# A one-core mixture-of-experts block: the two smallest of experts 2 to 7 as one fp32 job of 64 plus 64 slots

## The chip, the cores and the metric

The kernel runs on one core of one Trainium2 chip. The metric is the device time of one execution in microseconds, as the median of several runs. The profile is that of one execution, taken by the hardware profiler.

## What is computed

Four layers act on 256 tokens of 1024 features, all in fp32: a gated convolution and LRU mixer with a dense SwiGLU, the same mixer with a mixture of experts (MoE), an SSD and linear-attention layer, and an attention layer. The change touches the mixture of experts only:

```python
def moe_swiglu(h, w_router, wg, wu, wd):          # h: 256 x 1024
    logits = (xt @ w_router).astype(jnp.float32)   # 8 experts
    top_v, top_i = lax.top_k(logits, TOP_K)        # TOP_K = 2
    gates = jax.nn.softmax(top_v, axis=-1)
    ...
    for e in range(N_EXPERTS):                     # N_EXPERTS = 8, D_FF = 3584
        y = y + comb[:, e:e + 1] * swiglu(xt, wg[e], wu[e], wd[e])
```

Every token chooses two of eight experts, so 512 rows are spread over the experts. Worked out from the reference on its own inputs, experts 0 to 7 get 66, 73, 63, 66, 66, 56, 56 and 66 rows. The gate, up and down weights of one expert are 1024 x 3584, 1024 x 3584 and 3584 x 1024, 44 MB in all.

## The kernel before

**Pieces.** All weights come through one ring, `raw`, of RAW = 6 slots of 128 x 2048 fp32, one MiB each; a transfer of one MiB is called a piece here. SP issues the transfers in one order. `load` (L222 and on) lets SP wait until the piece six places earlier has been split (`w_lo`). ACT copies a piece in two halves to `whi`, rounded to fp32r (L558), and DVE subtracts to get the remainder `wlo` (L1079). `whi` and `wlo` have SPL = 3 places, so ACT can be three pieces ahead of TensorE, no more: it waits for `w_used`. `three` (L1848) then makes each product of three fp32r matmuls: high by high, high by low, low by high. For an expert a matmul has 128 slots as its stationary operand and 512 weight columns moving, so a piece costs 4 x 3 = 12 matmuls.

**Experts.** `gather` (L2101, L2102) picks up to 128 rows of each of two experts by one-hot matmuls, so a pair of experts is one `job_pair` of PU = 84 pieces. The hidden features are worked in blocks of 1024, 1024, 1024 and 512 (`FEAT`), eight steps to a pair. In step n TensorE does the gate pieces (banks 0 and 1), turns the hidden rows of the step before (`turn_h`, L2148, through banks 6 and 7), does the up pieces (banks 4 and 5), and then the down pieces of the step before (banks 2 and 3). ACT applies silu (L761) and evicts, DVE multiplies. Pieces of a 1024-wide block and all down pieces have runs of 4 KB in memory, those of the 512-wide gate and up blocks 2 KB.

**Order of the experts.** Pairs (0,1), (2,3), (4,5) and (6,7) run in this order, the last in a loop whose count is read from `tab`; an expert with more than 128 rows would add jobs to that loop. The results of jobs 0 to 3 are stored to `y_rows` in DRAM by GpSimd's queue (L488), fetched back by row number (L497) and added to X by DVE (L1441). Those of jobs 4 to 7 are scattered by one-hot matmuls (L2167, L2168). GpSimd works out the overflow and row tables (`overflow`, `two_rows`, L437 to L482).

**Elsewhere.** Three places of the trace show operations that resemble the new ones: `chunk_state` (L2289) and `att_out` (L2522, L2523) are plain fp32 matmuls of 128 x 64 stationary operands whose outputs go to partitions 0 to 63 and 64 to 127, and the router's logits (L2072) are fp32 matmuls of 8 columns, followed by `keep_busy` (L1968), which repeats transposes while DVE ranks the logits.

Of the kernel before, what the change touches and what calls it, by code (L numbers as in the profile page):

```python
# [24 lines left out]
P = 128  # L25
# [9 lines left out]
NJMAX = 12  # L35
# [18 lines left out]
STORED = 4  # L54
# [24 lines left out]
GATE, UP_, DOWN = step_units()  # L79

# [4 lines left out]
def build(nc, a, out):  # L85
    with ExitStack() as ctx:
# [40 lines left out]
        tab = sb("tab", [P, 6], I32)  # L127
        srt = sb("srt", [P, 1024], F32R)
        row_of = sb("row_of", [P, 2 * NT], I32)
        y_rows = nc.dram_tensor("y_rows", (STORED * P, D), F32, kind="Internal").ap()  # L130
# [51 lines left out]
        RV, VM, CW, RT = ar(936, NT, NE), ar(952, NT, NE), ar(968, NT, NE), ar(984, NT, NE)  # L182
        ROW = ar(1000, NT, 2)
        w_loaded = [sem(f"w_loaded{i}") for i in range(RAW)]
        w_hi, w_lo, w_used = sem("w_hi"), sem("w_lo"), sem("w_used")

        def plus(c, k, d):
            return c if isinstance(d, int) and d == 0 else d * k + c

# [35 lines left out]
        def _(sp):  # L225
            def load(u, src):
                c, d = u
                if c >= RAW or not isinstance(d, int):
                    sp.wait_ge(w_lo, plus(2 * (c - RAW + 1), 12, d))
                dst = raw[:, c % RAW, :]  # L230
                if len(src.shape) == 3:
                    dst = dst.rearrange("p (k n) -> p k n", k=src.shape[1])
                sp.dma_start(dst, src).then_inc(w_loaded[c % RAW], 16)
# [89 lines left out]
            def job_pair(e0, e1, d):  # L323

                for n in range(STEPS):
                    e = (e0, e1)[n // 4]
                    for m, units in ((eg, GATE[n]), (eu, UP_[n])):
                        for i, c in enumerate(units):
                            load((U_MOE + c, d), columns(m, e, i, n))
                    if n:  # L330
                        e = (e0, e1)[(n - 1) // 4]
                        for i, c in enumerate(DOWN[n - 1]):
                            load((U_MOE + c, d), down_rows(e, i, n - 1))
                for i, c in enumerate(DOWN[STEPS - 1]):
                    load((U_MOE + c, d), down_rows(e1, i, STEPS - 1))

            for p in range(NE // 2):
                job_pair(2 * p, 2 * p + 1, p * (2 * NG))
            sp.wait_ge(sem("tab_ready"), 1)
            njobs = sp.value_load(tab[0:1, 4:5], min_val=NE, max_val=NJMAX)  # L340
            npairs = sp.value_load(tab[0:1, 5:6], min_val=NE // 2, max_val=NJMAX // 2)
            with sp.If(njobs > NE):
                sp.wait_ge(sem("r_over"), 1)
                with sp.Fori(NE // 2, npairs) as p:
                    e0 = sp.value_load(tab[0:1, bass.ds(p * 2 - NE, 1)], min_val=0, max_val=NE - 1)
                    e1 = sp.value_load(tab[0:1, bass.ds(p * 2 - NE + 1, 1)], min_val=0, max_val=NE - 1)
                    job_pair(e0, e1, sp.snap(p * (2 * NG)))
# [34 lines left out]
        def _(pool):  # L382
# [45 lines left out]

            def overflow():

                pool.wait_ge(sem("r_log"), 1)
                pool.memset(TF[:, 0:4], 0.0)
                pool.memset(COMB[:, :, 11:14], 0.0)
                link(pool.memset(POS[:, :, 11:14], -1.0))
                pool.wait_ge(sem("r_step"), 4)
                G = GT3[:, 0, :].rearrange("p (e f) -> p e f", e=NE)
                link(pool.tensor_tensor(G, OV.unsqueeze(1).to_broadcast([P, NE, NE]), LTM[:, :].rearrange("p (e f) -> p e f", e=NE), ALU.mult))  # L437
# [5 lines left out]

                total(OVR.unsqueeze(2), lambda u, v: G[:, :, u:v])
                for m in range(3):
# [3 lines left out]
                    link(pool.tensor_tensor(EX, T16, sel2, ALU.mult))  # L449
                    total(MX.unsqueeze(2), lambda u, v: EX[:, :, u:v])  # L450
                    link(pool.tensor_scalar(POS[:, :, NE + m], MX, -1.0 - P, None, ALU.add))
                    link(pool.tensor_tensor(EX, COMB[:, :, 0:NE], sel2, ALU.mult))
                    total(COMB[:, :, NE + m:NE + m + 1], lambda u, v: EX[:, :, u:v])
                    link(pool.tensor_tensor(T8, SEL, iot[:, 0:NE], ALU.mult))
                    total(TF[:, m:m + 1], lambda u, v: T8[:, u:v])
                pool.tensor_copy(tab[:, 0:4], TF[:, 0:4]).then_inc(sem("r_over"), 1)

            def two_rows():

                def total4(o, x):  # L460

                    link(pool.tensor_tensor(RT[:, :, 0:2], x[:, :, 0:2], x[:, :, 2:4], ALU.add))
                    link(pool.tensor_tensor(o, RT[:, :, 0:1], RT[:, :, 1:2], ALU.add))

                first, second = RV[:, :, 0:4], RV[:, :, 4:8]
                valid, ahead, row = VM[:, :, 0:4], VM[:, :, 4:8], CW[:, :, 0:4]
                link(pool.memset(ahead, 0.0))
                link(pool.tensor_scalar(valid, T16[:, :, 0:STORED], float(P), None, ALU.is_le))
                link(pool.tensor_tensor(valid, valid, CH[:, :, 0:STORED], ALU.mult))
                for e in range(1, STORED):  # L470
                    link(pool.tensor_tensor(ahead[:, :, e:e + 1], ahead[:, :, e - 1:e], valid[:, :, e - 1:e], ALU.add))
                link(pool.tensor_tensor(second, valid, ahead, ALU.mult))
                link(pool.tensor_tensor(first, valid, second, ALU.subtract))
                link(pool.tensor_scalar(T8, iot[:, 0:NE], float(P), None, ALU.mult))
                link(pool.tensor_tensor(row, T16[:, :, 0:STORED], T8[:, 0:STORED].unsqueeze(1).to_broadcast([P, NT, STORED]), ALU.add))
                for k, m in enumerate((first, second)):
                    link(pool.tensor_tensor(CW[:, :, 4:8], COMB[:, :, 0:STORED], m, ALU.mult))
                    total4(WGT[:, :, k:k + 1], CW[:, :, 4:8])
                    link(pool.tensor_tensor(CW[:, :, 4:8], row, m, ALU.mult))
                    total4(ROW[:, :, k:k + 1], CW[:, :, 4:8])  # L480
# [3 lines left out]
            def rows_out_and_back():  # L484
# [4 lines left out]
                pool.wait_ge(sem("htok_lo"), 2)  # L489
                for b in range(2):  # L490
                    pool.wait_ge(sem(f"y_stored{b}"), 8 * STORED)
                for i in range(NT):
                    if i:
                        pool.wait_ge(sem("r_step"), 4 + i)
                    for k in range(2):
                        m = 2 * i + k
                        pool.indirect_dma_start(HTOK[:, k, :], None, y_rows[:, :],  # L497
# [4 lines left out]
            for k in range(10):  # L502
# [11 lines left out]
                if k == 3:  # L514
# [3 lines left out]
                    pool.tensor_tensor(HTOK[:, 0, :], X[:, 0, :], BG, ALU.mult).then_inc(sem("x_gain0"), 1)  # L518
# [12 lines left out]
                if k == 3:  # L531
                    overflow()
                    two_rows()
                    rows_out_and_back()
# [5 lines left out]
        def _(act):  # L540
# [8 lines left out]
            def split(u):  # L549
                c, d = u  # L550
                if c >= U_END:
                    return
# [2063 lines left out]
```

## Time and profile before

| | us |
|---|---|
| median of 3 runs | 1774.19 (1773.51 to 1774.86) |
| the profiled execution | 1774.9 |
| span of its profile | 1773.0 |
| TensorE busy | 1743.2 (98%) |
| weight loads of TensorE busy | 1479.7 (83%) |
| VectorE busy | 1409.8 (80%) |
| ScalarE busy | 1154.8 (65%) |
| granted TensorE clock, mean | 0.994 |
| moved by the DMA engines | 487.29 MB |

The profile is read with the names PE for TensorE, PEld for its weight loads, DVE for VectorE, ACT for ScalarE, POOL for GpSimd and SP for SyncE. L1848 is line 1848 of the kernel. A matmul's duration includes its way through the array, so in a row of matmuls the distance of the starts is the cost. A plain fp32 matmul is recorded as two. The DMA share is the mean busy share of the core's 16 DMA engines and can exceed 1 a little.

### The profile page before, as it was taken

The numbers are of one execution on the slowest core, as the hardware profiler recorded it, in microseconds if no ns is written. First come the engines' busy times: TensorE is split into PE (matmuls) and PEld (weight loads), VectorE is DVE, ScalarE is ACT, GpSimd is POOL, SyncE is SP. The second block draws the span as 40 slices with busy tenths as digits, with TensorE's granted clock in tenths as the row PEclk, the third lists the DMA queues.
The fourth block names the chain that finished last, engine by engine and source line by source line (L and its number), as shares of the span: only waits on it lengthen the run. The fifth ranks groups of instructions, "written<-read, shape, count | busy, mean of one in ns | idle before, by whom it ended". The sixth has DMA issues, their size and how long they took to land.

```text
span 1773.0 us, 23586 instructions
## 1 busy us (share of the span) xinstructions
PE 1743.2 (98%) x9169; PEld 1479.7 (83%) x9169; DVE 1409.8 (80%) x1532; ACT 1154.8 (65%) x1365; POOL 83.1 (5%) x137
## 2 busy tenths in 40 slices
PE   7999999999999999999999999999999999999998
PEld 7988888898888888888888888888888798778886
DVE  8864455697899998999989999989999888656555
ACT  5644444464777777777777777777777647554554
POOL 0000000001800000000000000000000001000000
PEclk9999999998999999999999999999999999999999
DMA  9555555544899999999999999999999834435420
GB/s 337 165 182 190 189 189 190 167 161 152 316 375 386 388 375 353 377 370 376 383 351 409 364 390 373 368 351 359 370 375 364 308 120 145 140 125 164 164 96 36
DMA packets 162734, 487.29 MB, mean 275 GB/s; under 512 B 13413, under 2 KB 14644, under 8 KB 162628
## 3 DMA queue, kind: packets, MB, share of 16 engines
q1 hardware_dynamic: 160832, 480.02, 74.2%
q0 software_dynamic: 1152, 4.19, 0.6%
q8 instruction: 70, 1.15, 0.3%
q10 hardware_dynamic: 644, 1.63, 0.2%
q14 instruction: 36, 0.29, 0.0%
HBM read 482.67 MB, written 3.15 MB: 274 GB/s over the span
## 4 chain that ended last, share of the span: by engine, by line
PE 93%; DVE 4%; ACT 1%; issue 1%; DMA 0%; POOL 0%; POOLq 0%; DVEq 0%; ACTq 0%
PE ps L1848 85%; PE ps L2148 1%; DVE wlo L1079 1%; DVE arena L1520 1%; PE ps L2101 1%; PE ps L2102 1%; DVE arena L1070 1%; ACT whi L558 0%; PE ps L1940 0%; PE ps L1992 0%; PE ps L2320 0%; PE ps L2035 0%; PE ps L2072 0%; PE ps L2512 0%; DMA X<-in_x 0%
## 5 line engine op out<-in xcount | busy, mean ns | idle before, releaser
L1079 DVE TENSOR_TENSOR wlo<-raw,whi 128x1024 fp32r<-128x1024 f32 x910 | 1067.9, 1221 | 236.2 <-ACT whi L558 232.7
L558 ACT ACTIVATE whi<-raw 128x1024 fp32r<-128x1024 f32 x910 | 913.4, 1053 | 455.7 <-PE ps L1848 453.8
L1848 PE MATMUL ps<-whi,ya 128*128 128x512 f32 x2272 | 715.8, 391 | 2.7 <-DVE ya L1070 1.4
L1848 PEld LDWEIGHTS ps<-whi,ya 128*128 128x128 f32 x2272 | 426.6, 188 | 91.1 <-issue 1.9
L1848 PE MATMUL ps<-wlo,ya 128*128 128x512 f32 x1136 | 442.2, 389 | 0.0
L1848 PE MATMUL ps<-whi,yh 128*128 128x512 f32 x896 | 281.9, 390 | 0.2
L1848 PEld LDWEIGHTS ps<-wlo,ya 128*128 128x128 f32 x1136 | 213.4, 188 | 43.1
L1848 PEld LDWEIGHTS ps<-whi,yh 128*128 128x128 f32 x896 | 168.2, 188 | 36.2 <-DVE yh L1070 1.2
L1848 PE MATMUL ps<-hhi,whi 128*128 128x256 f32 x656 | 188.2, 287 | 2.2 <-DVE hlo L1141 1.8
L1848 PE MATMUL ps<-hlo,whi 128*128 128x256 f32 x656 | 185.6, 283 | 0.0
L1848 PE MATMUL ps<-hhi,wlo 128*128 128x256 f32 x656 | 185.5, 283 | 0.0
L1848 PE MATMUL ps<-wlo,yh 128*128 128x512 f32 x448 | 174.3, 389 | 0.0
L1848 PE MATMUL ps<-whi,hhi 128*128 128x512 f32 x352 | 140.6, 399 | 0.8 <-DVE hlo L1141 0.8
L1848 PE MATMUL ps<-whi,hlo 128*128 128x512 f32 x352 | 137.4, 390 | 0.0
L1848 PE MATMUL ps<-wlo,hhi 128*128 128x512 f32 x352 | 137.1, 390 | 0.0
L1848 PEld LDWEIGHTS ps<-hhi,whi 128*128 128x128 f32 x656 | 125.6, 192 | 5.0 <-issue 4.1
L1848 PEld LDWEIGHTS ps<-hlo,whi 128*128 128x128 f32 x656 | 125.8, 192 | 0.1
L1848 PEld LDWEIGHTS ps<-hhi,wlo 128*128 128x128 f32 x656 | 125.7, 192 | 0.0
L1848 PEld LDWEIGHTS ps<-wlo,yh 128*128 128x128 f32 x448 | 84.1, 188 | 17.3
L1848 PEld LDWEIGHTS ps<-whi,hhi 128*128 128x128 f32 x352 | 66.2, 188 | 16.4 <-issue 2.9
L1848 PEld LDWEIGHTS ps<-whi,hlo 128*128 128x128 f32 x352 | 66.1, 188 | 14.1
L1848 PEld LDWEIGHTS ps<-wlo,hhi 128*128 128x128 f32 x352 | 66.2, 188 | 12.7
(369 smaller groups left out, 1133.0 us busy)
## 6 DMA issues: line engine op xcount, KB each, us to landing
raw<-in_moe_w_gate SPq DMA_DIRECT2D x112, 1024.0 KB, 7.2
raw<-in_moe_w_up SPq DMA_DIRECT2D x112, 1024.0 KB, 7.1
raw<-in_moe_w_down SPq DMA_DIRECT2D x112, 1024.0 KB, 7.5
raw<-in_even_w_in SPq DMA_DIRECT2D x21, 1024.0 KB, 5.1
raw<-in_w_in SPq DMA_DIRECT2D x20, 1024.0 KB, 6.0
raw<-in_odd_w_in SPq DMA_DIRECT2D x16, 1024.0 KB, 5.2
raw<-in_ffn_w_gate SPq DMA_DIRECT2D x14, 1024.0 KB, 5.1
raw<-in_ffn_w_up SPq DMA_DIRECT2D x14, 1024.0 KB, 5.1
```

The costliest lines, as they stand in the source:

```text
L558: act.activation(hi_of(u)[:, n], raw[:, c % RAW, n], ACT.Copy).then_inc(w_hi, 1)
L1070: return dve.tensor_tensor(o, x, y, op)
L1079: dve.tensor_tensor(lo_of(u)[:, n], raw[:, c % RAW, n], hi_of(u)[:, n].bitcast(F32), ALU.subtract).then_inc(w_lo, 1)
L1520: ins = dve.scalar_tensor_tensor(CVV[:, q, :], XP[:, q, k:k + S], col(1, C_ECONV + 10 * k + q), CVV[:, q, :], ALU.mult, ALU.add)
L1848: ins = pe.matmul(o, s, m, start=first and n == 0, stop=last and n == 2, skip_group_check=True)
L2101: pe.matmul(o, TKh[:, i, P * c:P * (c + 1)], SR[:, i, :], start=i == 0 and c % 2 == 0, stop=False)
L2102: ins = pe.matmul(o, TKl[:, i, P * c:P * (c + 1)], SR[:, i, :], start=False, stop=i == 1 and c % 2 == 1)
L2148: ins = pe.transpose(ps[:, 6 + q // 4, P * (q % 4):P * (q % 4 + 1)], MHF[:, P * q:P * (q + 1)], ident[:, :])
```

## The change

The two experts of 2 to 7 with the fewest rows are found on the chip. The other four and experts 0 and 1 keep the old path: three pairs, 252 pieces, in the order of a table that GpSimd makes. The two small experts form a job B. Its 84 pieces take no split: TensorE reads them from `raw` as plain fp32. The rows of one small expert stand in slots 0 to 63, those of the other in slots 64 to 127; each is a stationary operand of 64 columns whose output goes to its own half of the PSUM partitions. Job B is cut into 21 phases of four pieces (two of each expert), put in between the parts of pairs 0 and 1 by a table, from piece 24 on, some 6.1 pieces of the pairs apart (in fact 2, 4, 6 or 8); the last one comes after piece 150. Both kinds of pieces share the ring of six, fetched strictly in order of use, and a slot that held a B piece is freed by TensorE (`b_used`).

The phases use banks 6 and 7, so `turn_h` moves to banks 4 and 5, and ahead of the gate pieces of the next step. STORED falls from 4 to 3 (jobs 0 to 2 are stored), and job B's result is added up in SBUF (`YACC`) and stored as a fourth block. `add_rows` now runs in one go after pair 1. GpSimd gets the ranking of the experts (`jobs`) and a reordering of the tables; the overflow check is now against 128 rows for the six and 64 rows for the two small ones, and extra pairs run if it is exceeded.

```diff
-NJMAX = 12
+NJ0 = 6
+NJMAX = 10
-STORED = 4
+STORED = 3
+SLOTS = 5
+PHASES = [(kind, g, h) for g in range(4) for kind in "gud" for h in range(2 if g < 3 else 1)]
+LAST_HALF = [g == 3 or h == 1 for _, g, h in PHASES]
+FIRST_PHASE, PHASE_SPACING = 24, 6.1
+def load_order():
+    order, ahead = [], {done - 1: f for f, done in PHASE_AT.values()}
+    for a in range(2 * PU):
+        order.append(("A", a))
+        if a in ahead:
+            order += [("B", 4 * ahead[a] + i) for i in range(4)]
+        def load_wait(k, d):
+            if isinstance(d, int) and 0 <= k - U_MOE < len(ORDER):
+                kind, i = ORDER[k - U_MOE]
+                return (b_used, i + 1) if kind == "B" else (w_lo, 2 * (U_MOE + i + 1))
+            return w_lo, plus(2 * ((k if k < U_MOE else k - NB) + 1), 12, d)
...
# SP
+            eb, pieces = None, pair_pieces(0, 1)
+            for k, (kind, i) in enumerate(ORDER):
+                if eb is None and (kind == "B" or i == PU):
+                    sp.wait_ge(sem("router_made"), 2)
+                    eb = expert(10), expert(11)
+                if kind == "B":
+                    fetch(U_MOE + k, 0, small_piece(i, eb))
+                    continue
+                if i == PU:
+                    pieces = pair_pieces(expert(6), expert(7))
+                load((U_MOE + i, 0), next(pieces))
...
# ACT
+                f = PHASE_AT.get(here, (None,))[0]
+                if f is not None and PHASES[f][0] == "g" and LAST_HALF[f]:
+                    act.wait_ge(b_used, 4 * (f + 1))
+                    act.activation(HBC[:, 0:w], ps[:, 6:6 + w // 512, :]..., ACT.Silu).then_inc(sem("h_evicted"), 1)
...
# DVE
             def add_rows(i):
-                dve.wait_ge(sem("y_back"), 32 * (i + 1))
+                dve.wait_ge(sem("y_back"), 64)
...
# PE
+            def small_gather(half):
+                for i in range(NT):
+                    for c in range(4 * half, 4 * half + 4):
+                        pe.matmul(o, TKh[:, i, P * c:P * (c + 1)], m, start=i == 0 and c % 2 == 0, stop=False)
+                        ins = pe.matmul(o, TKl[:, i, P * c:P * (c + 1)], m, start=False, stop=i == 1 and c % 2 == 1)
+            def small_in(f, g, h):
+                for i in range(2):
+                    got = small_units(f, i)
+                    for k in range(ks):
+                        kk = ks * (2 * h + i) + k
+                        for b in range(width // 512):
+                            for s in range(2):
+                                pr, o = slice(64 * s, 64 * (s + 1)), width * k + 512 * b
+                                ins = pe.matmul(ps[pr, 6 + b, :], XBC[:, kk, pr], got[s][:, o:o + 512], start=kk == 0, stop=kk == KD - 1,
+                                                skip_group_check=True)
+                    ins.then_inc(b_used, 2)
...
-                    moe_in(GATE[n], d, n, 0, t if n == 0 else None)
+                    if n > 1:
+                        turn_h(t, n - 1)
+                    moe_in(GATE[n], u0, d, n, 0, t if n == 0 else None, (t, 0) if n == 1 else None)
+                    if not loop:
+                        small((t, n, "g"))
                     if n:
-                        turn_h(t, n - 1)
-                    moe_in(UP_[n], d, n, 4)
+                        pe.wait_ge(sem("m_htlo"), plus(n, STEPS, t))
+                    moe_in(UP_[n], u0, d, n, 4)
+                    if not loop:
+                        small((t, n, "u"))
...
-            for pair in range(STORED // 2):
-                job_pair(pair, pair * (2 * NG), 2 * pair + 1, stored=(2 * pair, 2 * pair + 1))
-            job_pair(STORED // 2, STORED * NG, STORED + 1, written=STORED)
+            job_pair(0, U_MOE, 0, 0, 1)
+            job_pair(1, U_MOE + PU, 0, 2, 3)
```

`small` puts a phase behind a part of a step: it gathers the small experts' rows once (`small_gather`, in step 1 of pair 0), turns the hidden rows of job B four times, and runs `small_in` for gate and up phases and `small_down`, of the same form, for down phases.

## Rows read from the trace of the kernel before

**Rows 1.** Stretches of 100 us: busy time (instructions), granted clock, DMA share, GB/s.

```profile
core 0: us, PE busy (x) PEld busy (x) DVE busy (x) ACT busy (x) POOL busy (x), PEclk, DMA share, GB/s
500.00:600.00 100.00, 100.00 (x457) 83.07 (x456) 91.30 (x84) 78.15 (x80) 0.81 (x1) 1.00 1.00 383
```

**Rows 2.** The same of the four pairs, and of all that follows.

```profile
443.00:683.00 240.00, 239.74 (x1100) 199.59 (x1101) 214.83 (x191) 183.60 (x187) 40.34 (x68) 1.00 0.97 365
683.00:921.00 238.00, 237.97 (x1094) 198.10 (x1093) 215.41 (x192) 183.90 (x188) 1.08 (x2) 1.00 0.99 375
921.00:1162.50 241.50, 241.43 (x1109) 200.54 (x1109) 224.15 (x204) 184.52 (x188) 6.44 (x5) 1.00 0.99 376
1162.50:1406.00 243.50, 243.35 (x1118) 202.06 (x1116) 224.31 (x205) 184.75 (x189) 0.00 (x0) 1.00 0.97 360
1406.00:1773.00 367.00, 351.83 (x2347) 302.56 (x2347) 242.75 (x377) 200.84 (x347) 18.76 (x18) 0.99 0.39 127
```

**Rows 3.** The chain that ended last, in order of time: start, us, what.

```profile
443.22 32.95 PE ps L1848 x144
476.18 0.87 PE ps L2148 x8
477.05 32.66 PE ps L1848 x144
...
672.43 0.44 PE ps L2148 x4
672.86 0.12 PE ps L2101
...
676.64 38.38 PE ps L1848 x168
...
1400.15 5.76 PE ps L1848 x24
1405.93 1.03 ACT yb L769
```

**Rows 4.** Waits from 440 to 1400 us, and of SP's queue from 500 to 1380 us.

```profile
ACT whi L558 <- PE ps L1848: 218.8, 298, 3.5
DVE wlo L1079 <- ACT whi L558: 71.2, 176, 3.1
...
SPq L233 <- DVE wlo L1079: 763.5, 309, 6.9
```

**Rows 5.** DMA issues by tensor: count, KB, median us to landing.

```profile
raw<-in_moe_w_gate SPq DMA_DIRECT2D x112, 1024.0 KB, 7.2
raw<-in_even_w_in SPq DMA_DIRECT2D x21, 1024.0 KB, 5.1
...
y_rows<-arena POOLq DMA_DIRECT2D x4, 512.0 KB, 7.6
...
arena<-y_rows,row_of POOLq DMA_INDIRECT x4, 8.3
```

**Rows 6.** Stretches of 5 and 10 us, columns as in rows 1.

```profile
10.00:15.00 5.00, 4.59 (x24) 4.22 (x25) 5.00 (x10) 4.65 (x10) 0.00 (x0) 1.00 1.04 382
15.00:20.00 5.00, 5.00 (x44) 5.00 (x43) 5.00 (x6) 3.43 (x5) 0.00 (x0) 1.00 1.05 387
...
630.00:640.00 10.00, 10.00 (x46) 8.29 (x45) 8.87 (x8) 7.96 (x10) 0.00 (x0) 1.00 0.95 347
690.00:700.00 10.00, 10.00 (x46) 8.29 (x45) 8.57 (x9) 8.04 (x9) 0.00 (x0) 1.00 1.03 417
```

**Rows 7.** PE in order of time around the 64-column fp32 matmuls: start, us.

```profile
1482.09 1.08 PE L2289 MATMUL ps<-arena,gb 128*64 128x512 f32 x4 [0.20 <-DVE arena L1070]
1483.10 0.50 PE L1848 MATMUL ps<-whi,hhi 128*128 128x512 f32 x1
...
1670.37 0.66 PE L2522 MATMUL ps<-gb,arena 128*64 128x256 f32 x4
1670.85 0.40 PE L2523 MATMUL ps<-gb,arena 128*64 128x128 f32 x4
1671.18 0.39 PE L1848 MATMUL ps<-hhi,whi 128*128 128x256 f32 x1
```

**Rows 8.** Groups from 440 to 1400 us: xcount, busy, mean ns, idle before.

```profile
L441 POOL TENSOR_TENSOR arena<-arena 128x4 f32<-128x4 f32 (+2 forms) x10 | 5.7, 567 | 0.8
...
L1441 DVE SCALAR_TENSOR_TENSOR X<-arena,X 128x1024 f32<-128x1024 f32 x4 | 5.1, 1283 | 0.1
```

**Rows 9.** PE in order of time, the router's matmuls: start, us.

```profile
424.62 5.29 PE L2072 MATMUL ps<-gb,hTf 128*128 128x8 f32 x32 [0.46 <-ACT hTf L735]
```

**Rows 10.** A stretch of 10 us behind them, columns as in rows 1.

```profile
430.00:440.00 10.00, 9.44 (x43) 8.79 (x43) 8.20 (x31) 2.39 (x4) 1.12 (x4) 0.50 0.00 1
```

More of the change, by code:

```diff
@@ L341, in _ @@
[L341 to L347, printed above, removed]
+                        for i in range(len(DOWN[n - 1])):
+                            yield down_rows(e, i, n - 1)
@@ new lines, in pair_pieces, with small_piece, expert @@
+                for i in range(len(DOWN[STEPS - 1])):
+                    yield down_rows(e1, i, STEPS - 1)
+            def small_piece(b, eb):
+                kind, g, h = PHASES[b // 4]
+                i = 2 * h + b // 2 % 2
+                return down_rows(eb[b % 2], i, g) if kind == "d" else columns((eg, eu)[kind == "u"], eb[b % 2], i, g)
+            def expert(o):
+                return sp.value_load(tab[0:1, o:o + 1], min_val=0, max_val=NE - 1)
+            eb, pieces = None, pair_pieces(0, 1)
@@ L458, in two_rows, with total5 @@
             def two_rows():
-                def total4(o, x):
+                def total5(o, x):
                     link(pool.tensor_tensor(RT[:, :, 0:2], x[:, :, 0:2], x[:, :, 2:4], ALU.add))
[L463 to L480, printed above, removed]
+                    link(pool.tensor_tensor(RT[:, :, 0:1], RT[:, :, 0:1], RT[:, :, 1:2], ALU.add))
+                    link(pool.tensor_tensor(o, RT[:, :, 0:1], x[:, :, 4:5], ALU.add))
@@ L789, in job_pair @@
                     if n == 4:
-                        used(U_MOE + DOWN[n - 1][-1], d)
+                        used(u0 + DOWN[n - 1][-1], d)
                         y0()
+                    if n and not loop:
+                        small((t, n, "d"))
                 ht_hi(t, STEPS - 1)
                 gath_hi(plus(1, 1, t))
-                after(U_MOE + DOWN[-1][0], d)
-                used(U_MOE + DOWN[-1][-1], d)
-                y1()
-                after(U_MOE + DOWN[-1][-1], d)
+                after(u0 + DOWN[-1][0], d)
@@ L1455, in job_pair @@
-                    if not stored and n in (1, 5):
-                        done = earlier if n == 1 else j1
-                        if done is not None:
-                            scatter(done)
-                            dve.wait_ge(sem("m_sev"), done)
+                    after(u0 + GATE[n][early], d, len(GATE[n]) - early)
+                    if n == 1 and not loop and t == 0:
+                        small_onehot()
+                    if not loop:
+                        small((t, n, "g"))
@@ L1460, in job_pair @@
+                    after(u0 + UP_[n][0], d, len(UP_[n]))
+                    used(u0 + UP_[n][-1], d)
+                    hid(t, n)
+                    if not loop:
+                        small((t, n, "u"))
+                    if loop and n in (1, 5):
+                        done = j0 if n == 1 else j1
+                        scatter(done)
+                        dve.wait_ge(sem("m_sev"), done)
+                    if loop and n == 1 or (loop or t) and n == 5:
                         weights_of(j0 if n == 1 else j1)
-                    if n == 2 and stored:
-                        dve.wait_ge(sem("m_gth"), 2 * t + 2)
+                    if n == 2 and not loop and t == 0:
+                        dve.wait_ge(sem("m_gth"), 2)
@@ L2108, in moe_in @@
+            def moe_in(units, u0, d, n, bank, fresh=None, turn=None):
                 s = n // 4
@@ L2199, in job_pair @@
                     if n:
-                        moe_down(t, d, n - 1)
+                        moe_down(t, u0, d, n - 1)
+                    if n and not loop:
+                        small((t, n, "d"))
                 turn_h(t, STEPS - 1)
                 gather(plus(1, 1, t))
-                moe_down(t, d, STEPS - 1)
-            for pair in range(STORED // 2):
-                job_pair(pair, pair * (2 * NG), 2 * pair + 1, stored=(2 * pair, 2 * pair + 1))
-            job_pair(STORED // 2, STORED * NG, STORED + 1, written=STORED)
```

495 lines of the change are left out of this document (356 added, 139 removed).

## The prediction

> **What bounds the kernel now.** I read the stretches of the span first, then the chain, then the waits, then the DMA rows. In the stretch of the experts TensorE is busy all the time at the full clock, and so, nearly, are the DMA engines: share 1.00 at 383 GB/s [rows 1]. VectorE is at 91%, ScalarE at 78%. So TensorE is the bound, but there are two resources near their end, and a change that relieves only one is worth what the other allows.
>
> The chain confirms it: from 443.2 to 1405.9 us it is TensorE's own work, with three-term matmuls in rows of 144 and a turn of hidden rows between [rows 3]. 144 matmuls take 32.66 us, 0.227 us each, so a piece of 12 costs 2.72 us, and 84 pieces 228.7. The four pairs are 240, 238, 241.5 and 243.5 us long [rows 2]; the 10 to 15 us above 228.7 are turns (0.87 us for 8), the gather (672.9 to 676.6, 3.7 us) and scatters. The waits show who is late: ScalarE waits for TensorE (218.8 us), VectorE for ScalarE, SP's queue for VectorE's split; nobody waits for a transfer [rows 4]. But a transfer of the experts lands 7.2 us after its issue, where a similar one in the slack stage lands after 5.1 [rows 5]: there is already a short queue. 84 MiB in 238 us are 370 GB/s at a share of 0.99 [rows 2].
>
> The span is thus 443.2 (before the experts) + 962.7 (four pairs) + 367.1 (all after) = 1773.0. It is 1.9 below the time of the profiled execution (1774.9) and 1.2 below the median (1774.19), so I add 1.2 to a span.
>
> **What the change takes and gives on TensorE.** It takes out one pair and puts 21 phases of 16 fp32 matmuls of 512 columns in. The cost of one is seen in `chunk_state`, of exactly this form: two such matmuls, on the two column blocks, start at 1482.09, and the next instruction starts at 1483.10, so both together cost 1.01 us, with the way in and out [rows 7]. Four of `att_out`, 256 and 128 columns on each block, cost 0.81 us (1670.37 to 1671.18). The difference, 128 columns, is 0.20, so in a row 512 columns of both blocks cost 0.80 from this difference and at most 1.01. I take 0.86, nearer the slope because eight pairs follow each other, plus 0.2 once: 7.1 us a phase (bounds 6.6 and 8.1). `att_out` writes both halves into one bank, as the phases do. 21 phases: 149 us for work that cost 228.7 us as split pieces.
>
> Further on TensorE: `small_gather`, 32 matmuls like the gather's, 3.7 us; 28 more transposes at 0.87/8, 3.1 us; one pair's turns, gather and scatter go. If nothing else bound it, the span would be 443.2 + 478 (pairs 0 and 1) + 149 + 3.7 + 3.1 + 2.5 (below) + 243.5 (the loop's pair) + 367.1 = 1690. A gain of 83 us, the most there is.
>
> **What the transfers allow.** The bytes stay: 336 pieces. Until now each had 2.72 us of TensorE to hide behind; in the mixed stretch, 126 pieces of the pairs (24 to 150) and 84 of job B, TensorE would need 126 x 2.85 (238/84 with the turns) + 149 = 508 us for 210 pieces, 2.42 us each, or 433 GB/s. No row reaches that. What can the queue deliver when always full? From below: share 1 at whole pairs means 376/0.99 = 380 and 360/0.97 = 371 GB/s [rows 2]. From above: 417 in the best 10 us, though 347 in a bad one [rows 6]. A full queue shows in the kernel's first microseconds, 382 and 387 at shares of 1.04 and 1.05, with runs of 2 KB, where the experts have mostly 4 KB. I take 390 GB/s: a piece (1.0486 MB) takes 2.69 us, bounds 2.51 (417) and 2.83 (371).
>
> Whole pairs ran at 375 and 376 GB/s [rows 2]. The Trainium skill, "DMA: Bandwidth & Descriptors", Specifications, gives about 358 GB/s as what one core can have from its memory and 435 as the ceiling of the fabric. By the first figure 206 pieces would take 604 us and the time below would be some 1790 in place of 1741; these two pairs already disagree with it, and no row comes near the second.
>
> The ring does not starve the engines in this state. While TensorE runs the last split piece ahead of a phase, SP can issue nothing from the second split piece behind the phase until two B pieces are used, about 3 x 2.72 + 3.5 - 2.3 (a split, ACT then DVE) = 9.4 us; but when transfers are the bound, five of six slots are under way then, over 13 us of transfer.
>
> The sum: 443.2; pieces 0 to 23, 24 x 2.72 = 65.3; two turns, 1.7; `small_gather` 3.7: TensorE reaches the first phase at 513.9. By then about 4 of the 210 pieces are there (six slots, 7.2/2.72 = 2.6 under way), so the last B piece comes 206 x 2.69 = 554.1 later, at 1068.0. Then TensorE needs the last half phase, 3.5, the 18 pieces 150 to 167, 49.0, three turns 2.2, the gather 3.8: 1126.5. Turns and the second gather of the mixed stretch cost nothing: TensorE has 2.69 x 210 - 508 = 57 us of waiting there, and if that cover were gone they are in the 508 already. The loop's pair is 243.5, the rest 367.1.
>
> **Smaller edits.** `add_rows` now runs 4 x 1.283 = 5.1 us in one go on VectorE [rows 8]; queued behind it are the splits for the loop's first pieces. Three pieces are split ahead, 8.2 us, less the 2.3 of a split in progress: between 0 and 5.1 us, I take 2.5. It waits for all four fetches, which wait for job B's store: last phase after piece 150, store and fetch 7.6 + 8.3 and the issues, some 22 [rows 5], while VectorE gets there 15 pieces later, over 40 us: 0. `jobs` on GpSimd puts 24 linked operations of about 0.57 us [rows 8] ahead of the table that SP needs for the first B piece: ready near 457, needed near 497: 0; if it were late, SP's queue would hold all weights behind it, up to as much as the delay. POOL has no weights to issue. ScalarE and VectorE lose 168 half splits each of 672, and gain some 8 evictions: no bound. Behind a phase their streams stand until the third next split piece has landed, so silu and the product come up to 12 us late; TensorE needs them after 2 to 4 more pieces, 5 to 11 us, mostly while it waits for that piece itself: 0, up to 1 us a phase. Register-addressed transfers already feed part of the dense layer: 0. The 56 rows of each small expert fit 64 slots and the 73 of the largest fit 128, so no extra pair runs.
>
> Span: 1126.5 + 2.5 + 243.5 + 367.1 = 1739.6, time 1740.8; 33 us, 1.9%, faster. With 2.51 us a piece it is 1704, with 2.83 it is 1770.
>
> **Rivals.**
> Transfers keep up (0.14): the phases' direct use of `raw` and deep queueing give over 405 GB/s; for it are stretches at 417 [rows 6], against it a pair's mean of 376. Time 1691 (TensorE alone) to 1718.
> The ring idles the DMA engines (0.08): if TensorE lags, all six slots land ahead of a phase, and the 9.4 us without an issue leave, say, 1.3 us idle each time: 21 x 1.3 = 27, time 1768. Against it: the reckoning above.
 Phases at 1.2 GHz take 14.2 us; with six pieces of the pairs, 17.1, that is 31.3 against 10 x 2.69 = 26.9 of transfer, so 21 x 4.4 = 92 more: 1833. It costs all the gain once a phase exceeds 26.9 - 17.1 + 33/21 = 11.4 us. Against it: 512-column phases keep the array busy, and `chunk_state` and `att_out` run amid full-clock stretches.
> The two column blocks do not overlap in long rows (0.03): 14 us a phase, 1833 too; both places of rows 7 speak against it.
> The memory gives less to a full queue than the pairs had (0.03): the fourth pair's 360 GB/s [rows 2] for good would make a piece 2.91 us, 206 of them 600, the time 1787; the gain is gone from 2.69 + 33/206 = 2.85 us a piece, 368 GB/s. Against it, that pair ran at a share of 0.97 and two others at 375 and 376. It is the case that the Trainium skill's figure (same page and section) would bring about.
> No change to be told (0.04).
>
> **How the numbers follow.** The likeliest case (0.60) is 1718 to 1770 with 1741 at its middle. From 1700 to 1769 the range leaves out the fastest part of the first rival and all cases of loss, some 0.2. About 0.2% (3.5 us) is what this measurement can tell from no change. Faster 0.82, same 0.04, slower 0.14.
>
> **What would show it.** In the profile after: DMA share at or over 1.0 and 385 to 395 GB/s from about 510 to 1070; TensorE busy below 95% there, waiting for B pieces and for VectorE's split, which waits for ScalarE, which waits for a transfer; landing times well over 7.2 us; phases 7 us long; the last phase near 1070, the end of the third pair near 1372; the clock at 1.00. Wrong, if the share is under 0.95 with TensorE waiting (the ring), if the clock falls, or if phases take over 8.1 us.

## The result: faster by 0.65%, a third of what was forecast

The changed kernel takes 1763.66 us in the median of 5 runs (1758.63 to 1765.52), the kernel before 1774.21 (1773.51 to 1774.86). The ratio is 0.9935, 95% interval 0.9919 to 0.995. The forecast was 1741 with a range of 1700 to 1769, so the time lies in the range and the sign was right, but of 33 us forecast only 10.5 came.

The span is 1761.6 us against a forecast of 1739.6, 22.0 more. Cut at the same places as the sum:

| stretch | forecast | measured |
|---|---|---|
| up to the first phase | 513.9 | 512.2 |
| from there to the end of the last phase ("mixed stretch") | 557.6 | 567.4 |
| from there to the last piece of pair 1 ("tail") | 55.0 | 66.4 |
| from there to the last piece of the loop's pair | 246.0 | 250.1 |
| the rest | 367.1 | 365.6 |

The forecast of the mixed stretch was 206 x 2.69 and 3.5 for the last half phase, that of the tail 49.0 + 2.2 + 3.8. The measured marks are these pieces of the chain of the changed kernel (start, us, what). L2068 is the three-term matmul, L2363 and L2377 are job B's matmuls, L714 is ScalarE's split and L1267 VectorE's. L1257 is VectorE's helper for everything that takes two operands: `yh` are the remainders of a pair's hidden rows, `arena` the products of the hidden rows.

```profile
512.20 7.02 PE ps L2363 x32
...
1042.10 7.02 PE ps L2363 x32
1049.12 11.20 PE ps L2068 x48
1061.63 10.91 PE ps L2068 x48
1076.17 6.85 DMA raw<-in_moe_w_up
1087.63 4.57 DVE wlo L1267 x5
1092.20 17.80 DMA raw<-in_moe_w_up
1114.66 19.47 PE ps L2068 x72
1140.48 5.48 PE ps L2068 x24
1157.33 20.96 PE ps L2068 x84
...
1390.54 5.48 PE ps L2068 x24
```

The last phase starts at 1072.5, behind the matmuls of 1061.63, and ends at 1079.6. A phase costs 7.0 us, 32 records for 16 matmuls, where 7.1 was forecast. The chain is no longer TensorE's alone, as in [rows 3]: it passes through transfers, splits and evictions.

The stretches, columns as in [rows 1] (the second is a part of the first; the first and third answer to the first three of [rows 2]):

```profile
512.00:1079.00 567.00, 524.99 (x2333) 349.23 (x2332) 327.76 (x296) 280.31 (x289) 13.62 (x37) 0.98 0.98 385
600.00:700.00 100.00, 86.54 (x384) 57.27 (x381) 57.31 (x50) 50.03 (x52) 0.82 (x1) 0.97 0.93 369
1079.00:1146.00 67.00, 59.07 (x265) 47.63 (x262) 52.65 (x47) 43.60 (x46) 6.48 (x5) 0.95 1.00 396
1394.00:1762.00 368.00, 351.86 (x2356) 301.72 (x2354) 244.36 (x378) 202.30 (x349) 18.78 (x18) 1.00 0.38 127
```

In the mixed stretch TensorE is idle for 42 of 567 us, and the transfers run at 385 GB/s, near the forecast's 390, but at a share of 0.98, and of 0.93 from 600 to 700. The waits from 440 to 1400 us (total, times, longest) say for whom it waits; they answer to [rows 4]:

```profile
ACT whi L714 <- DMA raw<-in_moe_w_gate: 132.7, 33, 11.5
ACT whi L714 <- PE ps L2068: 99.0, 115, 5.8
ACT whi L714 <- DMA raw<-in_moe_w_down: 81.4, 36, 11.9
...
PE ps L2068 <- DVE wlo L1267: 14.3, 13, 3.2
...
PE ps L2068 <- DVE yh L1257: 9.8, 4, 5.2
...
PE ps L2325 <- DVE yh L1257: 8.9, 3, 5.2
...
PE ps L2377 <- ACT arena L938: 8.5, 1, 8.5
...
PE ps L2452 <- DVE arena L1257: 5.1, 2, 3.5
```

ScalarE now waits mostly for transfers, which is the forecast's picture. But three of TensorE's four longest sums are waits for an eviction (hidden rows `yh`, job B's copy L938), not for weights; so is that of L2452, the turn of a pair's hidden rows. A gate transfer lands after 9.0 us where it was 7.2 [rows 5]:

```profile
raw<-in_moe_w_gate SPq DMA_DIRECT2D x112, 1024.0 KB, 9.0
```

### The profile page after: what moved, and what is told of

It reads as the page before. It is cut to its first block, busy times and chain, and to the rows that moved or that the text cites. A ratio compares the mean times of both kernels' runs of the same rounds, so it can differ in the third digit from the quotient of the medians.

```text
span 1761.6 us, 22930 instructions
## 1 busy us (share of the span) xinstructions
PE 1677.6 (95%) x8797; PEld 1335.3 (76%) x8797; DVE 1197.5 (68%) x1342; ACT 977.0 (55%) x1187; POOL 119.8 (7%) x215
## 4 chain that ended last, share of the span: by engine, by line
PE 77%; DVE 9%; DMA 9%; ACT 3%; issue 2%; POOL 0%; DVEq 0%; POOLq 0%; SPq 0%; ACTq 0%
PE ps L2068 66%; DVE wlo L1267 5%; DMA raw<-in_moe_w_up 4%; PE ps L2363 3%; DMA raw<-in_moe_w_gate 3%; PE ps L2377 2%; ACT whi L714 2%; DMA raw<-in_moe_w_down 2%; DVE arena L1257 1%; DVE arena L1740 1%; PE ps L2452 1%; DVE yh L1257 1%; PE ps L2212 0%; PE ps L2632 0%; PE ps L2160 0%
## 5 line engine op out<-in xcount | busy, mean ns | idle before, releaser
L1267 DVE TENSOR_TENSOR wlo<-raw,whi 128x1024 fp32r<-128x1024 f32 x742 | 871.2, 1222 | 436.6 <-ACT whi L714 434.5
L714 ACT ACTIVATE whi<-raw 128x1024 fp32r<-128x1024 f32 x742 | 744.7, 1053 | 616.8 <-PE ps L2068 331.9
L2068 PE MATMUL ps<-whi,ya 128*128 128x512 f32 x1824 | 582.5, 395 | 20.7 <-DVE yh L1257 9.8
L2068 PEld LDWEIGHTS ps<-whi,ya 128*128 128x128 f32 x1824 | 346.2, 190 | 103.9 <-DVE yh L1257 11.7
L2068 PE MATMUL ps<-wlo,ya 128*128 128x512 f32 x912 | 358.3, 393 | 0.0
L2068 PE MATMUL ps<-whi,yh 128*128 128x512 f32 x672 | 213.5, 392 | 5.4 <-DVE wlo L1267 5.4
L2068 PEld LDWEIGHTS ps<-wlo,ya 128*128 128x128 f32 x912 | 173.2, 190 | 34.4
L2068 PE MATMUL ps<-hhi,whi 128*128 128x256 f32 x656 | 188.2, 287 | 2.5 <-DVE hlo L1329 2.2
L2068 PE MATMUL ps<-hlo,whi 128*128 128x256 f32 x656 | 185.6, 283 | 0.0
L2068 PE MATMUL ps<-hhi,wlo 128*128 128x256 f32 x656 | 185.6, 283 | 0.0
L2068 PEld LDWEIGHTS ps<-whi,yh 128*128 128x128 f32 x672 | 126.6, 188 | 37.3 <-DVE wlo L1267 7.4
L2068 PE MATMUL ps<-whi,hhi 128*128 128x512 f32 x352 | 140.6, 399 | 0.8 <-DVE hlo L1329 0.8
L2068 PE MATMUL ps<-whi,hlo 128*128 128x512 f32 x352 | 137.4, 390 | 0.0
L2068 PE MATMUL ps<-wlo,hhi 128*128 128x512 f32 x352 | 137.1, 390 | 0.0
L2068 PE MATMUL ps<-wlo,yh 128*128 128x512 f32 x336 | 131.1, 390 | 0.0
L2068 PEld LDWEIGHTS ps<-hhi,whi 128*128 128x128 f32 x656 | 125.9, 192 | 5.2 <-issue 4.4
L2068 PEld LDWEIGHTS ps<-hlo,whi 128*128 128x128 f32 x656 | 125.9, 192 | 0.1
L2068 PEld LDWEIGHTS ps<-hhi,wlo 128*128 128x128 f32 x656 | 125.9, 192 | 0.0
L2363 PE MATMUL ps<-raw,arena 128*64 128x512 f32 x448 | 100.4, 596 | 4.8 <-DMA raw<-in_moe_w_gate 3.2
L2363 PEld LDWEIGHTS ps<-raw,arena 128*64 128x64 f32 x448 | 31.6, 137 | 66.2 <-issue 66.2
L2068 PEld LDWEIGHTS ps<-whi,hhi 128*128 128x128 f32 x352 | 66.2, 188 | 16.4 <-issue 2.9
L2068 PEld LDWEIGHTS ps<-whi,hlo 128*128 128x128 f32 x352 | 66.1, 188 | 14.2
```

Of the source, the lines that this page charges most:

```text
L714: act.activation(hi_of(u)[:, n], raw[:, k % RAW, n], ACT.Copy).then_inc(w_hi, 1)
L1267: dve.tensor_tensor(lo_of(u)[:, n], raw[:, k % RAW, n], hi_of(u)[:, n].bitcast(F32), ALU.subtract).then_inc(w_lo, 1)
L2068: ins = pe.matmul(o, s, m, start=first and n == 0, stop=last and n == 2, skip_group_check=True)
L2363: ins = pe.matmul(ps[pr, 6 + b, :], XBC[:, kk, pr], got[s][:, o:o + 512], start=kk == 0, stop=kk == KD - 1, skip_group_check=True)
```

## The experiments

Two theories stood against each other. Theory 1: the transfers are the bound, with nothing else to blame. Theory 2: a wait that the forecast priced at nothing, that of evictions behind a split in the in-order streams of ScalarE and VectorE. Times of experiments with one run have no interval.

### Half of job B's bytes; then an eighth of its matmuls' columns

```diff
-                    fetch(U_MOE + k, 0, small_piece(i, eb))
+                    whole = small_piece(i, eb)
+                    fetch(U_MOE + k, 0, whole[:, 0:whole.shape[1] // 2, :])
```

> The transfer of each of job B's 84 pieces is cut to its first half (0.5 MiB), so the kernel multiplies stale data in the other half; all instructions stay. Theory 1, transfers are the bound of the mixed stretch (567 us after): 42 MiB less, 42 x 2.6 = 109 us less transfer, so TensorE's own 508 us become the bound, 50 to 60 us less: span 1705 to 1715. Theory 2, waits of the in-order streams (evictions behind a split whose piece comes after the phase) and the add_rows block are what cost: the waits stay but landings come earlier, 10 to 25 us less: 1735 to 1752.

1722.29 us (one run), 41 less than after. The first phase to the end of the last takes 527.8 us instead of 567.4. The time lies between the two expected ranges and in neither. The other edit leaves all transfers and thins the matmuls of job B:

```diff
-                                ins = pe.matmul(ps[pr, 6 + b, :], XBC[:, kk, pr], got[s][:, o:o + 512], ...
+                                ins = pe.matmul(ps[pr, 6 + b, 0:64], XBC[:, kk, pr], got[s][:, o:o + 64], ...
```

> Each matmul of job B takes 64 of its 512 columns (the rest of the result is left out), so a phase costs about 1.5 us of TensorE instead of 7.1; all transfers and waits stay. Theory 1 (transfers bound): 336 pieces must still come, time within 15 us of after, span 1745 to 1761. If TensorE and its waits set the time, 21 x 5.6 = 117 us minus what transfers then allow: below 1730.

1748.53 us (one run), 15 less than after, and TensorE is busy for 431 of the 548 us of the mixed stretch. The stretches of the two kernels, half the bytes first:

```profile
512.00:1039.00 527.00, 516.44 (x2332) 346.47 (x2328) 332.31 (x299) 282.91 (x291) 14.25 (x37) 0.99 0.87 335
```

```profile
513.00:1061.00 548.00, 430.85 (x2334) 346.95 (x2332) 327.47 (x295) 279.02 (x287) 18.42 (x36) 0.89 1.01 397
```

Taking 94 us off TensorE's busy time (525 to 431) brings 19 us in the stretch, and there the DMA share is 1.01; taking away 42 MiB brings 40. So the transfers are the floor, at 548 us or somewhat less (this run still has a wait of 7.1 us for job B's copy), and the changed kernel is not on it. With half the bytes TensorE still is not fully busy (516 of 527) at a DMA share of 0.87: a second wait exists. Both theories hold a part.

### Evictions first

In the changed kernel ScalarE does the splits of a whole part, three pieces ahead of TensorE, and only then the part's evictions. With a phase behind that part, the third piece stands behind job B's four in the ring. The edit puts the evictions ahead of the last split, wherever a phase starts up to two pieces behind the part (`HOLD`); the work is the same.

```diff
+HOLD = parts_before_phase()
...
-                    after(u0 + UP_[n][0], d, len(UP_[n]))
+                    after(u0 + UP_[n][0], d, len(UP_[n]) - hu)
                     if not loop:
                         small((t, n, "u"))
+                    after(u0 + UP_[n][-1], d, hu)
...
+                    if n and hd:
+                        ht_hi(t, n)
+                        turned.add(n)
+                        after(u0 + DOWN[n - 1][-1], d, 1)
```

> Same work. In the parts of pairs 0 and 1 that end up to two pieces ahead of a phase, ScalarE and VectorE do the evictions (silu, hidden rows, job B's silu and copy) ahead of the split of the part's last piece in their order, no longer behind it; that piece is fetched after job B's four. Theory 2 (order of the streams): the waits of TensorE for ScalarE's copy (8.5 us in one place) and for VectorE's hidden rows (9.8 us in four) go, and with them some of the half clock: 10 to 25 us less than after, 1738 to 1754. Theory 1 (transfers alone): within 4 us of after.

1746.49 us (1745.8 to 1748.13), ratio to before 0.9846, interval 0.983 to 0.9863: 17 us less than after. This is called the mended kernel below. Its mixed stretch is 551.0 us, its tail 66.3:

```profile
513.00:1064.00 551.00, 522.59 (x2334) 346.87 (x2332) 329.07 (x298) 281.38 (x290) 13.27 (x34) 0.99 1.01 397
1064.00:1130.00 66.00, 58.15 (x261) 47.59 (x260) 50.51 (x45) 42.25 (x44) 6.83 (x5) 0.95 1.01 397
```

What the wait looks like in the changed kernel, in its chain and in TensorE's order of time:

```profile
597.21 8.60 DMA raw<-in_moe_w_up
...
614.99 11.46 DMA raw<-in_moe_w_gate
626.50 0.94 issue
627.44 1.04 ACT whi L714
628.48 0.92 ACT arena L938
629.44 8.67 PE ps L2377 x32
```

```profile
629.44 8.67 PE L2377 MATMUL ps<-raw,arena 128*64 128x512 f32 x32 [8.45 <-ACT arena L938]
```

```profile
625.00:633.00 8.00, 3.56 (x10) 1.15 (x12) 5.44 (x5) 4.81 (x5) 0.00 (x0) 0.57 0.23 93
```

TensorE stands before the first down phase and waits for ScalarE's copy of job B's hidden rows (L938). Its weights are long there, and so is what L938 copies: the transposes for it ended at 615.5. ScalarE has it queued behind the split (L714) of the piece that lands last. Meanwhile the slots of job B's pieces are not freed, so the DMA engines run dry too, at a share of 0.23 in these 8 us. The granted clock is 0.57 in them, and the phase takes 8.67 us instead of 7.02. With evictions first the same phase starts at 620.98:

```profile
620.98 7.09 PE L2411 MATMUL ps<-raw,arena 128*64 128x512 f32 x32
```

SP's queue, which must wait for these slots, says the same. Its waits for the down matmuls of job B from 500 to 1150 us, before and after the mend (total, times, longest):

```profile
SPq L304 <- PE ps L2377: 76.7, 14, 17.1
```

```profile
SPq L321 <- PE ps L2411: 66.1, 14, 7.7
```

What the order costs in the mixed stretch is thus transfer time. Both kernels move the same there (567 us at 385 GB/s and 551 us at 397, 218 and 219 MB), and the engines are busy for some 556 us in both (0.98 of 567, 1.01 of 551); so the 16 us between them are, within the rounding of the shares, idle time of the DMA engines. Taken in stretches of 4 us against a share of 1.02, they fall short by 27 us in the changed kernel and by 11 in the mended one (an estimate from the traces), and 9 of the difference lie between 624 and 640, at this one wait.

The Trainium skill ("TensorE: Matmul & The Clock Gate", Architectural detail) says that ScalarE's and VectorE's queues are strictly first in, first out. The trace agrees: a copy of 0.92 us whose operand had been ready since 615.5 started at 628.48, behind a split, and TensorE waited for it for 8.45 us.

### Only job B's evictions first

> Only job B's own evictions (silu, copy, product, sum) go ahead of the split of the part's last piece; the pairs' silu, hidden rows and their remainders stay behind it. If the 8.5 us wait of the first down phase for ScalarE's copy is the main cost of the order, most of the 17 us of evictions first is there: 1749 to 1755. If the pairs' hidden rows cost as much, half of it: 1754 to 1759. Baselines: 1763.66 after, 1746.49 evictions first.

1756.16 us (1754.48 to 1758.83), ratio 0.9901, 0.9884 to 0.9917. Of 17 us, 7.5 come from job B's own evictions and the other 10 from those of the pairs, each to within some 4 us (the runs of this kernel and those of the changed one nearly touch). The expectation gave two ranges, 1749 to 1755 and 1754 to 1759; it is the second: both kinds count, about evenly. TensorE's direct waits for the pairs' hidden rows, from 510 to 1082 us, fit: 14.9 us after, 19.5 in this run, 5.2 in the mended kernel.

### Evictions first, with half the bytes

> Evictions first, and job B's pieces transferred by half (stale data in the other half). With the order mended and transfers relieved, only TensorE is left: the mixed stretch 510 to 515 us against 551, time 1700 to 1710. If some other wait (the ring's order, the hidden rows) still costs, 1712 to 1722, near the 1722.29 of the half transfers alone.

1711.51 us (one run):

```profile
513.00:1025.00 512.00, 511.40 (x2333) 344.14 (x2332) 334.94 (x299) 286.28 (x292) 11.42 (x36) 1.00 0.89 345
1025.00:1091.00 66.00, 57.98 (x264) 46.70 (x263) 48.19 (x43) 39.93 (x42) 5.89 (x5) 0.97 1.01 398
```

TensorE is busy for 511.4 of 512: its own time, forecast at 508. So with the order mended and the transfers relieved, no third wait is left in the mixed stretch, which lies in its expected range. The time, 1.5 us above the expected 1700 to 1710, does not: the tail is as long as ever, 66 us.

### One matmul of three for the pairs

```diff
+            def one(o, xh, xl, wh, wl, first, last, weights_stationary):
+                return pe.matmul(o, xh, wh, start=first, stop=last, skip_group_check=True)
```

> The kernel after, with one matmul in place of three for each product of pairs 0 to 2 (high by high; the two others are left out), so a piece of them takes 0.9 us of TensorE; splits, transfers and job B stay. What the queue delivers when it is never waited for by TensorE: if 404 GB/s (as in windows with a full queue), 252 pieces take 654 us and the mixed stretch of 208 pieces 540 us; if 385, 566 us. The loop's pair is then bound by VectorE's splits or by transfers, 84 x 2.44 to 2.6 = 205 to 220 us: span 1690 to 1725.

1721.14 us (one run). The mixed stretch:

```profile
500.00:1057.00 557.00, 421.46 (x1324) 180.01 (x1320) 329.24 (x297) 280.61 (x290) 36.05 (x86) 0.78 1.00 394
```

557.8 us from the first phase to the end of the last, with two thirds of the pairs' matmuls gone: TensorE is idle for 136 of 557 us, and the transfers run at 394 GB/s at a share of 1.00. The expectation named 404 or 385 GB/s; it is between them, and the forecast's 390 is right to 1%. That the stretch is as long as the forecast's 557.6 us is chance: it holds the bytes of 210 pieces and not 206 (394 GB/s for 557.8 us), and the wait for job B's copy (L938) is still in it, 11.3 us long. The granted clock is 0.78 here; what it costs can't be read from this run, where TensorE has a third of the pairs' matmuls.

### One column block

The mended kernel, with both halves of job B put out to the same partitions, in gate, up and down phases:

```diff
-ps[pr, 6 + b, :]
+ps[0:64, 6 + b, :]
```

> Evictions first, but both small experts' outputs go to partitions 0 to 63 (the result of one is lost), so that the two matmuls of a pair share a column block and cannot overlap. A phase should take 14 us in place of 7.09. Then TensorE needs 508 + 149 = 657 us for the mixed stretch against 551: time 1850 or so, slower than before. If 64-column fp32 matmuls on one block took no longer than on two, the time would stay at 1746.

1848.78 us (one run). A phase takes twice as long, and TensorE is busy all of 654 us, the DMA share at 0.88:

```profile
512.30 13.88 PE ps L2397 x32
```

```profile
512.00:1166.00 654.00, 654.00 (x2333) 388.15 (x2332) 334.81 (x299) 286.03 (x293) 10.57 (x37) 1.00 0.88 336
```

So the overlap of the two column blocks is real, worth 6.9 us a phase; without it the kernel takes 102 us more than the mended one and 75 more than the kernel before. The forecast's price for this rival, 1833, is within 16 us.

### The tail: `add_rows` and the rows' traffic

First the two halves of `add_rows` were moved into step 7 of pair 1:

```diff
+                    if n == 7 and not loop and t == 1:
+                        add_rows(0)
...
-            for i in range(NT):
-                add_rows(i)
```

> Same work. The two halves of add_rows stand in step 7 of pair 1 instead of behind the pair. It takes away TensorE's wait of 3.2 us and the 3.4 us at half clock behind it: 3 to 6 us less than after if that block is on the path; no change if the transfers only give the wait another place.

1762.44 us (1761.56 to 1767.13), ratio 0.9946, 0.9929 to 0.9964: no difference to after that can be told. Behind the mended order:

> Evictions first and add_rows in step 7 of pair 1, together. Evictions first alone measured 1746.49, add_rows early alone 1.2 us less than after. If the transfers set the time up to the end of pair 1, DVE's block costs where it stands behind the pair (3.2 us of TensorE's wait and half clock after it) and moving it gives 2 to 5 us: 1741 to 1745. If its rows arrive too late for the new place, 0 or worse.

1749.34 us (1747.08 to 1750.19), ratio 0.9861, 0.9844 to 0.9877, against 0.9846 without the move; the two intervals overlap. The trace shows where the wait goes. This is the chain just ahead of the gather behind pair 1:

```profile
1113.47 9.08 DVE wlo L1293 x8
1122.55 1.21 DVE X L1650
1123.76 0.02 issue
1123.79 1.28 DVE X L1650
1125.07 0.61 DVE yh L1283
```

TensorE no longer waits 3.2 us behind `add_rows` (L1650), but the gather waits for `yh`, which now stands behind its second half: 5.7 us in both runs, 1.9 without the move. Then the traffic was left out, on top of evictions first, so that `add_rows` adds what stands in its buffers:

```diff
-                pool.dma_start(y_rows[P * STORED:P * (STORED + 1), :], YACC).then_inc(sem("y_stored1"), 16)
...
-                        pool.indirect_dma_start(dst, None, y_rows[:, :],
-                                                bass.IndirectOffsetOnAxis(ap=row_of[:, m:m + 1], axis=0)).then_inc(sem("y_back"), 16)
```

> Evictions first, and the store of job B's block and the four fetches by row number are left out (add_rows adds what stands in the buffers). 2.5 MiB less behind the last phase, 6.5 us at 404 GB/s. If this traffic is what makes the tail (last phase to the end of pair 1) 66 us instead of 55, the tail loses 6 to 11 us: time 1736 to 1741. If the tail is long because TensorE starts it with no piece ahead, under 3 us: 1744 to 1747.

1740.71 us (1738.78 to 1740.98), ratio 0.9814, 0.9797 to 0.983. The tail falls from 66.3 to 57.1 us, TensorE busy for 55:

```profile
1063.00:1120.00 57.00, 54.92 (x262) 45.52 (x262) 50.47 (x46) 41.86 (x45) 0.00 (x0) 1.00 1.03 406
```

6 us of time, 9 of the tail (some 3 of them come back in later stretches): 2.5 MiB of rows share the same engines with the weights just when TensorE has no piece in hand. The longest wait of the tail's chain for one transfer is 12.3 us here; it is 17.8 in the changed kernel (at 1092), 18.7 in the mended one and 19.2 with half of job B's bytes. Behind that piece's split stand hidden rows once more. TensorE waits for them before the last up pieces of pair 1, in the changed kernel, in the mended one (whose `HOLD` does not reach this part; the second line is the sum of two waits, the longest is this one) and, without the rows, no more than 0.19 us:

```profile
PE ps L2068 <- DVE yh L1257: 5.2, 1, 5.2
```

```profile
PE ps L2102 <- DVE yh L1283: 6.2, 2, 5.1
```

```profile
1090.21 1.15 DVE yh L1274
1091.36 0.04 issue
1091.40 16.63 PE ps L2095 x72
```

The same 72 matmuls take 19.47 us in the changed kernel, behind the wait of 5.2 us: from 1115 to 1120 the granted clock is 0.50.

### Phases closer together

The mended kernel once more:

```diff
-FIRST_PHASE, PHASE_SPACING = 24, 6.1
+FIRST_PHASE, PHASE_SPACING = 24, 5.2
```

> Evictions first, with the phases 5.2 instead of 6.1 pieces apart: the last one stands behind piece 132, so 36 pieces of the pairs follow without job B. If transfers set the time of the mixed stretch and TensorE's 2.72 us a piece that of the rest, the sum hardly moves: within 4 us of 1746.5. If closer phases meet more waits of the ring and the streams, 5 to 15 us slower than that.

1746.53 us (1746.19 to 1749.64), ratio 0.9855, 0.9839 to 0.9871. Up to the end of the last phase 502.5 us, from there to the end of pair 1 another 114.0, together 616.5; with the wider spacing 551.0 + 66.3 = 617.3. The place of the phases is neutral, as it must be if transfers are the bound up to the end of pair 1; they run at 396 and 401 GB/s in the two stretches, at a share of 1.01. The rows' traffic now has up to 36 pieces to hide behind, the wait of 5.1 us for hidden rows is gone, and yet the sum is the same. So the 2.5 MiB cost their transfer time wherever they stand: at 397 GB/s they take 6.6 us, an estimate that fits the 6 us of the run without them.

## Why the prediction was wrong in size

**Right.** The bound, and where the gain would stop. The queue's rate with a full ring was taken as 390 GB/s between 371 and 417; the kernel with thinned pairs shows 394, the mended kernel 397, and its mixed stretch of 551.0 us is 206 pieces at 2.66 us and half a phase, where 2.69 was forecast. The Trainium skill's 358 GB/s for one core ("DMA: Bandwidth & Descriptors", Specifications) is again not what the trace shows: 397 over 551 us. A phase costs 7.0 us, not 7.1; TensorE's own time of the stretch is 511.4, not 508; `jobs` was in time: the first phase came 1.7 us before its forecast. The stretch behind the experts was 1.5 us shorter.

**The step that failed** is among the smaller edits: "Behind a phase their streams stand until the third next split piece has landed, so silu and the product come up to 12 us late; TensorE needs them after 2 to 4 more pieces, 5 to 11 us, mostly while it waits for that piece itself: 0, up to 1 us a phase." The mechanism was seen and priced at nothing. Mending just this order gives 17 us, 0.8 us for each phase, near the upper end that was named and then left out of the sum. Two things were overlooked in it. First, a late eviction is not hidden in TensorE's waiting for weights: job B's pieces are at the head of the ring and need no split, so when a phase itself waits for an eviction (8.45 us before the first down phase), its slots stay taken and the DMA engines run dry, at a share of 0.23. The transfers being the bound, what they lose there is never got back; by the estimate above it is 9 of the 16 us of the mixed stretch. Second, the new place of `turn_h` ahead of the gate pieces makes TensorE wait for the hidden rows (`m_htlo`) before the up pieces; in the steps of 512 features only two gate pieces lie between, 5.4 us, and an eviction 12 us late is then on the path: 4.6 us in three places of the mixed stretch, and 5.2 in a fourth, in the tail. The turn itself waits 5.1 us for the pairs' products, and the gather between the pairs 5.2 us. Of the 14.9 us of the mixed stretch (4.6, 5.1 and 5.2) 9.7 go with the mend; that fits the 10 us that the pairs' evictions brought, but the two were not tied wait by wait.

**The term of the tail** was too small by 11.4 us. It counted TensorE's work only; in the trace TensorE waits there for 7.9 us (5.2 for the hidden rows above, 1.9 ahead of the gather, 0.8 for a split), and the half clock behind the first of them costs 3.1 (19.47 against 16.33 for 72 matmuls). The rows' store and fetch were priced as latency ("VectorE gets there 15 pieces later: 0"), which was right, and not as bytes in a queue that was said to be full. Without them the tail is 57.1 us, 2 above the forecast.

**`add_rows`** cost more than the 2.5 us taken: TensorE waited for 3.2 us behind it, and the 84 matmuls at 1157.33 took 20.96 us instead of 19.05, the first of them at half clock. Together that is 5.1 us, by chance the upper bound that was named, which left the clock out. Moving it to where it was tried gained nothing that can be told, since the wait for `yh` ahead of the gather grew by 3.8 us, as much as was won behind it. The loop's pair as a whole took 250.1 us, 4.1 more than forecast; the other 1.5 us above these 5.1 were not traced.

**The sum:** the 22.0 us are 9.8 in the mixed stretch, 11.4 in the tail and 4.1 in the loop's pair, less 1.7 and 1.5 before and behind. In the mixed stretch the order cost 16.4 us (567.4 to 551.0), and a rate a little better than forecast gave 6.6 back. Of the tail's 11.4, 9.2 go with the bytes of the rows. With the order mended the time is 1746.5, 5.7 above the forecast.

**The rivals.** That the ring idles the DMA engines (0.08, 1768) comes nearest, and its sign was there: a share of 0.93 from 600 to 700 with TensorE waiting. What set it off was not foreseen: a late eviction holds the slots, or makes TensorE lag, and then, as the trace reads, a phase meets a full ring (the share is 0.10 from 804 to 808, right behind the start of a phase at 803). The time without an issue by itself costs little: SP's queue waits up to 10.2 us in the mended kernel too, whose share is 1.01. The clock (0.08) did fall in the changed kernel, to 0.97 in two stretches of 100 us, but behind waits of TensorE; the phases took 7.0 to 7.4 us where no transfer held them up, but for the one of 8.67 behind the wait of 8.45. Its part in the mixed stretch was not measured by itself. TensorE was busy there for 525.0 us, against 511.4 with the same matmuls at a clock of 1.00 (evictions first, half the bytes), so it is at most 13.6 us of TensorE's time, and 11.2 of them are in the mended kernel too, under transfers at a share of 1.01. Transfers did not keep up with TensorE, and the memory gave no less to a full queue than before (385 to 397 GB/s against 376). The column blocks overlap.

**What stays open.** Whether the evictions put first in the tail too would gain anything, with the transfers at a share of 1.01 there; whether `add_rows` in another place than those tried would; and what the half clock costs by itself. The runs with half the bytes, the thinned ones and that with one column block are single ones, but the differences read from them are 15 us and more.

## What to carry to other kernels

When a change relieves one of two resources near their end, the gain stops at the other, and from there on a moment in which that other one has nothing to do is lost for good: look for what can hold its slots. In an in-order engine that both prepares work ahead and clears results, put the clearing ahead of a preparation whose input is fetched later than the next consumer. Count the bytes of side traffic, not only its latency, once the queue is full.

## What the runs showed of the hardware

Two plain fp32 matmuls of 128 x 64 stationary operands on the two column blocks ran fully at once in rows of eight pairs: 7.0 us for 16 of 512 columns, 13.9 us when both used one block. Each reads its own moving operand, and both wrote one PSUM bank. The DMA engines with a full ring gave 394 to 397 GB/s over 550 us and 406 over 57 us (share 1.03). The share is no measure of room: it was 0.97 to 0.99 at 360 to 376 GB/s before [rows 2], and the same engines then gave 397.
